# A two-layer fp32 trunk on one core: the second half's first two head tiles side by side, its mean ahead of them, identity matmuls in the wait

## The reference

```python
def sandwich_in(h, m, sub, p):
    return rms_norm(h, p['norm_pre'][sub]) * (1 + m[:, 3 * sub + 1]) + m[:, 3 * sub]
def sandwich_out(h, y, m, sub, p, weight):
    return h + weight * m[:, 3 * sub + 2] * rms_norm(y, p['norm_post'][sub])
def swiglu(h, wg, wu, wd):
    return (jax.nn.silu(h @ wg) * (h @ wu)) @ wd
```

## Time and profile before

| | us |
|---|---|
| median of three runs | 2881.44 |
| profiled execution, own time | 2880.92 |
| its span, first to last instruction | 2879.1 |
| TensorE busy | 2757.3 |
| VectorE busy | 1978.8 |
| ScalarE busy | 1099.0 |
| GpSimd busy | 794.7 |
| mean granted TensorE clock | 0.986 |

### The profile page before, as it was taken

One profiled execution on the slowest core, in us unless ns is written; L12 is line 12 of the kernel. 1 busy time (PEld: TensorE's weight loads), 2 busy tenths in 40 slices (PEclk: granted clock), 3 DMA queues, 4 the chain that ended last, 5 costly groups with the idle time before them and its releaser, 6 DMA issues.

```text
span 2879.1 us, 44629 instructions
## 1 busy us (share of the span) xinstructions
PE 2757.3 (96%) x17104; PEld 2636.1 (92%) x17104; DVE 1978.8 (69%) x3402; ACT 1099.0 (38%) x1898; POOL 794.7 (28%) x609
## 2 busy tenths in 40 slices
PE   6999999999999899999999999999999998899998
PEld 5999999988878889999999899999988877899997
DVE  4877888667345778989886888778657447654434
ACT  3312324453353452324245333324454534522234
POOL 3700313150043275312225821313240123400002
PEclk8999999999999999999999999999999999999999
DMA  7454443452221352443525433443442412453333
GB/s 234 138 151 133 137 132 94 141 152 58 92 58 34 107 157 77 126 136 87 147 82 153 150 107 108 134 132 88 147 142 61 128 41 81 134 146 96 89 93 113
DMA packets 468351, 332.25 MB, mean 115 GB/s; under 512 B 36150, under 2 KB 419484, under 8 KB 467628
## 3 DMA queue, kind: packets, MB, share of 16 engines
q1 hardware_dynamic: 459568, 304.65, 37.0%
q10 hardware_dynamic: 8572, 24.74, 2.4%
HBM read 312.11 MB, written 17.22 MB: 114 GB/s over the span
## 4 chain that ended last, share of the span: by engine, by line
PE 75%; DVE 12%; issue 4%; ACT 4%; POOL 3%; DMA 2%; SPq 0%; ACTq 0%; DVEq 0%; POOLq 0%
PE ps L2337 22%; PE ps L2339 22%; PE ps L2338 22%; ACT wsp L1076 2%; DVE macc L1657 2%; DVE wsp L1613 2%; POOL scr L857 2%; PE ps L2805 2%; PE ps L2780 2%; PE ps L2781 2%; DVE hn L1722 1%; PE ps L2792 1%; ACT hn L1131 1%; POOL wsp L866 1%; DMA raw<-in_ffn_w_gate 1%
## 5 line engine op out<-in xcount | busy, mean ns | idle before, releaser
L2337 PE MATMUL ps<-hn,wsp 128*128 128x384 f32 (+1 forms) x2400 | 780.2, 325 | 33.2 <-DVE hn L1722 23.5
L2338 PE MATMUL ps<-hn,wsp 128*128 128x384 f32 (+1 forms) x2400 | 772.1, 322 | 0.0
L2339 PE MATMUL ps<-hn,wsp 128*128 128x384 f32 (+1 forms) x2400 | 771.5, 321 | 0.0
L1613 DVE TENSOR_TENSOR wsp<-raw,wsp 128x1024 fp32r<-128x1024 f32 (+2 forms) x304 | 344.3, 1133 | 323.5 <-ACT wsp L1076 322.3
L2337 PEld LDWEIGHTS ps<-hn,wsp 128*128 128x128 f32 x2400 | 456.4, 190 | 49.9 <-issue 17.0
L1076 ACT ACTIVATE wsp<-raw 128x1024 fp32r<-128x1024 f32 (+2 forms) x344 | 325.0, 945 | 461.8 <-PE ps L2339 288.7
L2338 PEld LDWEIGHTS ps<-hn,wsp 128*128 128x128 f32 x2400 | 456.9, 190 | 0.0
L2339 PEld LDWEIGHTS ps<-hn,wsp 128*128 128x128 f32 x2400 | 456.7, 190 | 0.0
L2337 PE MATMUL ps<-aT,wsp 128*128 128x384 f32 (+1 forms) x1344 | 439.9, 327 | 14.1 <-DVE wsp L1613 5.6
L2338 PE MATMUL ps<-aT,wsp 128*128 128x384 f32 (+1 forms) x1344 | 433.9, 323 | 0.0
L2339 PE MATMUL ps<-aT,wsp 128*128 128x384 f32 (+1 forms) x1344 | 433.9, 323 | 0.0
(11 more groups left out here) (297 smaller groups left out, 4741.9 us busy)
## 6 DMA issues: line engine op xcount, KB each, us to landing
modw<-in_w_mod SPq DMA_DIRECT2D x144, 512.0 KB, 3.9
raw<-in_ffn_w_gate SPq DMA_DIRECT2D x188, 256.0 KB, 3.4
raw<-in_ffn_w_up SPq DMA_DIRECT2D x188, 256.0 KB, 4.1
raw<-in_ffn_w_down SPq DMA_DIRECT2D x96, 256.0 KB, 3.1
raw<-in_ffn_w_down SPq DMA_DIRECT2D x128, 192.0 KB, 2.7
raw<-in_w_in SPq DMA_DIRECT2D x96, 256.0 KB, 3.1
raw<-in_w_out SPq DMA_DIRECT2D x64, 256.0 KB, 3.2
spill<-xT ACTq DMA_DIRECT2D x4, 3072.0 KB, 10.4
```

Source lines behind the costliest of these rows:

```text
L1613: dve.tensor_tensor(wsp[:, t % 2, 1, 0:width], raw[:, t % RAW, 0:width], wsp[:, t % 2, 0, 0:width].bitcast(F32), ALU.subtract).then_inc(wl ...
L2337: pe.matmul(dst, w(0), x(0), start=first, stop=False)
L2338: pe.matmul(dst, w(0), x(1), start=False, stop=False)
L2339: return pe.matmul(dst, w(1), x(0), start=False, stop=last)
```

## The change

Twelve edits in one:

1. For half 1 the first two head tiles are worked side by side (`head_pair`): blocks 0, 1 of tile 0, blocks 0, 1 of tile 1, blocks 2, 3 of tile 0, and so on. Tile 1 goes to bank 0, so ScalarE empties bank 0 ahead of `pre` (step "first": the Silu of the first gate, or the copy of the first mixer feature).
2. `mean` and `spread` of half 1 stand before blocks 4 and 6 of the fourth tile, not 6 and 8.
3. 3 identity matmuls of 128 columns (5 for 256-wide halves) stand between the fourth tile and the pair (`warm`).
4. The weights of the second and third head tile of half 1 are split in two pieces: rows 0 to 3 early ("fore": ScalarE, GpSimd) once those rows of the slot have been used, the rest later.
5. In a SwiGLU block ScalarE's and VectorE's steps after the pair are reordered.
6. For half 0 the last square is not added by GpSimd; `mean` sums it with one more matmul per 128 tokens (`single`), in all leads but the first.
7. `columns` moves from ahead of `last_pass` to behind its second tile; ScalarE splits the first two weights ahead of the squares.
8. `input_hi`/`input_lo` of `tA` move behind the half chunk.
9. At the mixer's end blocks 0 to 3 of the first two `w_out` tiles are worked before the transposes of blocks 4 to 7 (`mixed_part`), and their `mix_hi`/`mix_lo` come earlier.
10. Head 2's norm of the first triple is summed by ScalarE (`spread_of_values`); VectorE's moments for both last heads' second triple move into `last_pass`.
11. At the start: mean of half 1 early, spread before block 2, the first two tiles of half 0 side by side too (`first_pair`), and 5 + 7 identity matmuls around that mean.
12. Waits and small matmuls of the mixer's lead are moved to fit.

The core of the diff:

```diff
-HEAD_BANKS = [[0, 2, 4, 5], [6, 3, 0, 2]]
+HEAD_BANKS = [[0, 2, 4, 5], [6, 0, 3, 2]]
     "ACT": [("mean", 1, 1), ("head", 0), ("xsq", 1, 0), ("xsq", 1, 2), ("head", 1), ("xsq", 1, 4), ("xsq", 1, 6),
-            ("head", 2), ("mean", 0, 1), ("head", 3)] + [("pre", 1, k) for k in PAIRS],
-    "POOL": [("head", 0)] + [("xsq", 1, k) for k in PAIRS[:3]] + [("head", 3)],
-    "PE": {(0, 5): ("mean", 1, 1), (0, 6): ("spread", 1, 1), (3, 6): ("mean", 0, 1), (3, 8): ("spread", 0, 1)},
+            ("head", 2), ("fore", 0), ("mean", 0, 1), ("first",), ("pre", 1, 0), ("head", 3), ("pre", 1, 2),
+            ("pre", 1, 4), ("fore", 1), ("pre", 1, 6)],
+    "POOL": [("head", 0)] + [("xsq", 1, k) for k in PAIRS[:3]] + [("fore", 0), ("head", 3), ("fore", 1)],
+    "PE": {(0, 5): ("mean", 1, 1), (0, 6): ("spread", 1, 1), (3, 4): ("mean", 0, 1), (3, 6): ("spread", 0, 1)},
...
+            def warm(bank, count):
+                for _ in range(count):
+                    pe.matmul(ps[:, bank, 0:P], ident, ident, start=True, stop=True)
+            def head_pair(l, sub, n, ready, free):
+                t = first_tile0(l, sub) + HEAD * n
+                a, w = halves_of(l, sub, 0)[n]
+                for k in range(0, KD, 2):
+                    for i in range(2):
+                        if (k, i) == (0, 1) and free is not None:
+                            pe.wait_ge(*free)
+                        for kk in (k, k + 1):
+                            rows_split(t + i, kk)
+                            if i == 0:
+                                ready(kk)
+                            ins = three(ps[:, HEAD_BANKS[n][i], 0:w], weight((t + i) % 2, kk * P),
+                                        lambda p: normal(p, kk, a, w), kk == 0, kk == KD - 1)
...
                 if paired(l, sub, post, n, KD - 1):
                     pe.wait_ge(pair_done, pairs_at(l, sub))
                     sums.append(pair2[0])
+                if single(l, sub, post, n, KD - 1):
+                    pe.wait_ge(sq_done, SQ_AT[l, sub, post, n, KD - 1] + 1)
+                    sums.append(pair2[0])
...
                 mix_turns(0, range(HEADS))
                 for d in range(2):
                     head_out(last, 1, d)
-                mix_turns(0, range(HEADS, KD))
+                pe.wait_ge(mo_out, out_no(l, last, 0) + 1)
+                for dt in range(2):
+                    mixed_part(l, dt, True)
+                mix_turns(0, range(HEADS, KD), 3)
                 return lambda k: mix_turns(1, LATE[k])
...
             mod0_turn(3)
+            warm(HEAD_BANKS[0][3], 5)
+            mean(0, 0, 0, 1)
+            warm(HEAD_BANKS[0][3], 7)
```

More of the change, by code:

```diff
@@ L282, in first_tile0, with fore_no, split_from @@
 def first_tile0(l, sub): return mix_tile0(l) if sub == 1 else ffn_tile0(l, sub // 2)
+FORE = KD // 2 * P
+def fore_no(t):
+    for l in range(L):
+        for sub in range(3):
+            i = t - first_tile0(l, sub) - HEAD - 1
+            if (l, sub) != (0, 0) and i in (0, 1):
+                return 2 * (3 * l + sub - 1) + i
+    return None
+def split_from(t): return 0 if fore_no(t) is None else FORE
 def split_by_pool(t):
@@ L2222, in mixer @@
                 memory_out(l, last, 0)
+                for k in range(HEADS):
+                    mix_lo(0, k)
+                inverse(1, tts, 1)
                 dve.wait_ge(o_outs, o_before(l) + len(tts))
@@ L2226, in mixer @@
                 variance(last, triples(l)[0])
-                inverse(1, tts, 1)
-                moments(last - 1, tts)
-                variance(last - 1, tts)
-                for k in range(2):
-                    mix_lo(0, k)
-                inverse(last, triples(l)[0], 2)
-                inverse(2, tts, 3)
-                for k in range(2, HEADS):
-                    mix_lo(0, k)
+                inverse(2, triples(l)[0], 2)
                 memory_out(l, last, 1)
+                inverse(last, triples(l)[0], 3)
                 gated(last, 1)
@@ L2414, in mix_input, with output @@
                 return mix[p][:, k, a:a + w]
-            def output(bank, cs, G, a, w, x, ready=None, half=False):
+            def output(bank, cs, G, a, w, x, ready=None, half=False, halfway=None):
                 for k in range(G):
@@ L2428, in output @@
                                 k == 0, k == G - 1)
+                    if halfway is not None and k == KD // 2 - 1:
+                        ins.then_inc(halfway, 1)
                 ins.then_inc(unit_done, 1)
@@ L2466, in active, with mixed_part @@
                 return ready
+            def mixed_part(l, dt, first):
+                a, w = halves_of(l, 1, 1)[0]
+                t = last_tile0(l, 1) + dt
+                if first:
+                    pe.wait_ge(wlo_done, splits_before(t) + 1 + RAW)
+                    pe.wait_ge(yadd_done, last_down0(l, 1) + dt + 1)
+                for k in range(HEADS) if first else range(HEADS, KD):
+                    pe.wait_ge(mlo_done, 16 * l + k + 1)
+                    ins = three(ps[:, 4 + dt, 0:w], weight(t % 2, k * P), lambda p: mix_input(p, k, a, w),
+                                k == 0, k == KD - 1)
+                if not first:
+                    ins.then_inc(unit_done, 1)
             def head(l, sub, n, k, ready):
@@ new lines, in first_pair @@
+            def first_pair(ready):
+                a, w = halves_of(0, 0, 0)[0]
+                h = KD // 2
+                for i, ks in ((0, range(2)), (1, range(2)), (0, range(2, h)), (1, range(2, h)), (0, range(h, KD)),
+                              (1, range(h, KD))):
+                    for k in ks:
+                        if k == 0:
+                            pe.wait_ge(wlo_done, splits_before(i) + 1 + RAW)
+                        if i == 0:
+                            ready(k)
+                        ins = three(ps[:, HEAD_BANKS[0][i], 0:w], weight(i, k * P), lambda p: normal(p, k, a, w),
+                                    k == 0, k == KD - 1)
+                    if ks[-1] == KD - 1:
+                        ins.then_inc(unit_done, 1)
```

292 lines of the change are left out of this document (196 added, 96 removed).

## The result

The changed kernel takes 2863.22 us (median of 4 runs, 2859.73 to 2863.42), the one before 2881.57 in the same session (2881.25 to 2883.2): a ratio of 0.9932, 95% interval 0.9915 to 0.995. The forecast was 2840 us with a range of 2827 to 2856. The direction was right, the size was less than half of it: 18.4 us gained where 41.3 were expected. The profiled execution took 2863.24 us with a span of 2861.4; before it was 2880.92 and 2879.1.

What follows compares the result with a forecast made beforehand. TensorE, busy 96% of the span, was taken as the bound, with its stops and half-clock stretches. Gains of 22.1 + 1.7 + 4.9 + 0 + 9.6 + 3.0 = 41.3 us off 2880.9, plus 0.5, gave 2840 us; range 2827 to 2856.

Steps and rivals of the forecast that it cites:

- Part 1: Five leads behind the first: VectorE sets the pace, paired tiles fill TensorE's stops; 22.1 us gained, bounds 12 to 24.
- The cover that I called thin: Leads, third tile's lower split half and fourth tile: ready 0.5 us ahead of need, loss set at nothing.
- rival B: Half 1's third or fourth tile and later ones wait for weight splits: 10 us lost, 2850 us; chance 0.16.
- Rival A: TensorE's clock stays low in the leads: 11 us lost over four, 2851 us; chance 0.11.
- Rival D: GpSimd's half splits block VectorE's `pre` in the leads: slower than before, 2884 us at 3.0 each; chance 0.03.
- A silent drain at the table load: ScalarE in three leads: skill's drain of about 1380 ns per switch would cut 3 us; forecast trusted the trace, no cost.
- Part 2 and 3: Half 0's means without GpSimd's last addition, 1.7 us; SwiGLU third output tile's weight wait goes, 4.3 us.
- Part 3 in the mixers: Second mixer: a wait of 1.6 us goes, 1.0 given back for moments and columns behind the second tile.
- Part 4: `tA` behind the half chunk, group 0: shorter low-part wait, later first evacuation; net nothing, -5 to +5 us.
- Part 5: Mixers' ends: matmuls fill the waits and moments move; 5.8 and 3.8 us, 9.6 in all, bounds 5 and 16.
- Part 6: The start: VectorE's chain loses two pauses, 3.5 us; taken as 3 us, bounds 0 and 8.
- the two-piece order: At the start: said to keep TensorE from adding a tile at the end, within the 3 us taken there.

Runs made afterwards that it cites:

- e5: Changed kernel without the identity matmuls ahead of the pair in the five leads behind the first: 2859.36 us against 2863.2.
- e4: Changed kernel with half 1's head tiles one behind the other again in the five leads behind the first, all else kept: 2873.35 us against 2863.2.
- e3: Changed kernel with columns ahead of the last pass again in the two mixers only: 2858.59 us against 2863.2.
- e2: Changed kernel with tA's split ahead of the half chunk again, as before the change: 2857.3 us against 2863.2.
- e11: Changed kernel run again unaltered, as yardstick; its trace is the "second profile": 2861.86 us.
- e14: Against the kernel with three losses undone (2848.3 us): last four of GpSimd's forty input sums per block done over only 8 columns: 2844.3 us.
- e15: Against the kernel with three losses undone (2848.3 us): GpSimd's last eight input sums wait until behind the half chunk's last low part: 2854.93 us.

## Why the prediction was wrong

**Part 1, right.** The leads' lengths came out within 0.12 us each (22.6 us together against 22.1), by VectorE's rhythm as the chain. The cover that I called thin was: in two SwiGLU leads TensorE waits 0.96 us for a split. That split takes 2.03 us beside GpSimd's sums, as it did before the change (2.04 us), so the old trace had the duration and my cover of 0.5 us was too small for it. To "leave the loss at nothing" was the mis-sized term: of the 22.6 us 18.2 are left once the tiles behind the leads are counted in, 4.4 us off in all, of which the two waits are 1.9. It is the beginning of rival B. Rival A fell, the clock was 1.00: e5 shows that the identity matmuls aren't needed for it and e4 that they aren't enough without the pair. Rival D fell too: two of VectorE's steps of `pre` take 1.14 us as before. A silent drain at the table load is not there either: 69.23 + 1.28 = 70.51, and the Silu begins at 70.53.

**Part 2 and 3 in the SwiGLU blocks, right.** The third output tile no longer waits, the means of half 0 have 12 records and no wait of 1.13; 8.8 us against 6.0 with the rest (6.7 in the second profile).

**Part 3 in the mixers, mis-sized.** I set 1.0 us for "moments and columns now load VectorE behind the second tile", and for the second mixer alone. The waits are 2.07 and 2.76 us, and e3 takes out 3.5. The 0.98 us that the first of the columns took was no part of my sum.

**Part 4, wrong, 11.3 us with what it stands for (6.9 in the second profile).** That "the first evacuation of the group comes behind that split instead, and TensorE waits for it" was named, and set to nothing because I took the two waits to be alike. The evacuation has two copies of columns (1.3 us) and the split (1.76) ahead of it, and of the old wait 0.92 is left; this cost about 3 us over three blocks (e2 against e11, with a clock fall in e2 counted off). Some 3 more are clock falls. The rest no part had: the leads take TensorE 4 us forward and GpSimd 2, so that GpSimd's sums of the input now end inside the chain that closes group 0 and hold up VectorE's splits (e14, e15); by e14 this cost 1.5 us in the third block, and in the second its size is mixed with a clock fall. The same stands behind the third block, where the four additions ahead of the turn take 5.82 us beside GpSimd's sums of weights and TensorE waits 1.8 (4.81 and 0.78 in the second profile); no run tested this one.

**Part 5, right.** 22.32 - 16.29 = 6.0 us and 15.98 - 12.65 = 3.3, 9.3 against 9.6. The clock fell again, for 3.4 us each and not 10 (6.8 in the first mixer of the second profile).

**Part 6, wrong, and the largest miss with a single cause: 7.7 us.** I wrote that "the two-piece order keeps TensorE from adding a tile at the end" and looked at the first lead's half 0 alone. The pair of half 1 needs a bank that in this block nothing frees; that the banks of tiles 1 and 2 were exchanged (an edit of one line) and that FIRST has no "first" stood in the diff. With the pair out of the first block, part 6 holds: 4.4 us against 3.

With three of the losses undone the kernel is at 2848.3 us, inside the range; the change as written had them.

## What to carry to other kernels

When tiles are interleaved so that one can hold the other, list for each what it needs to start (bank, split, input) in every place where the pair runs, the first block too, whose lists differ. When a stretch is shortened by filling TensorE's waits, ask how much shorter it is for the engine that set the pace, and which engine beside it (here GpSimd, with 55 us of sums) keeps its own time: the two then meet at a new place, their instructions hold each other up, and durations from the old trace are too short there. A split put "behind" something should be followed to the next instruction behind it on its own engine.

## What the runs showed of the hardware

One kernel profiled twice gave 2863.24 and 2859.36 us. Most of the difference lies in stretches of 3.4 us at the lower of the two clock levels while TensorE is busy throughout, which one execution has and the other hasn't (144.4 and 1127.4 us above); each of these costs 1.5 to 1.6 us. The one at 1127.4 us begins 0.6 us behind a wait of 2.48 us, and the same wait stands in the execution without it. Single profiles of this kernel can't tell less than about 4 us apart by their total, while each of the five leads, compared by itself, repeats to 0.03 us.

VectorE's instructions with two inputs in SBUF took up to 0.82 us longer beside GpSimd's sums (640 columns 1.64 for 0.82 us, 1536 columns 2.57 for 1.76), and its evacuations from PSUM took 0.55 us beside them (e15, at 1119.50) as elsewhere.
